# A decoder layer on one core: the mixer's output projection as seven products of quadrants instead of eight, and one weight split moved to the change of head pairs

## The chip, the cores and the metric

The kernel runs on one core of a Trainium2 chip, as one program. The metric is the time of the device in microseconds (us); lower is better. The profile was taken of one execution. TensorE (PE) multiplies, VectorE (DVE) and ScalarE (ACT) work on tiles in SBUF and PSUM, GpSimd (POOL) does small sums and issues some DMAs, SyncE (SP) issues most DMAs.

## The reference, cut to what matters

```python
def reference(x, mem, ...):
    h = rmsnorm(x, norm_mix_g)
    u_pool, q, k, v, f_logit, g_logit = jnp.split(h @ w_in, IN_SPLITS, axis=-1)
    y_pool = pool_mixer(u_pool, pool_w, pool_scale) @ w_pool_out
    y_fox = forgetting_attention(q, k, v, f_logit + b_forget) @ w_fox_out
    g_pool, g_fox = ...                                  # sigmoid gates, (1024, 1024) each
    x = x + (g_pool * y_pool + g_fox * y_fox) @ w_out    # the projection that is changed
    x = x + memory_cross_attention(rmsnorm(x), rmsnorm(mem), w_xq, w_xkv, w_xo)
    x = x + (silu(gt) * up) @ w_ffn_out                  # gt, up = rmsnorm(x) @ w_ffn_in
    return rmsnorm(x)
```

There are 1024 tokens, the model is 1024 wide, and all is float32. Call z = g_pool * y_pool + g_fox * y_fox. The changed product is z @ w_out, 1024 x 1024 by 1024 x 1024.

## The kernel before

Every float32 operand is kept as two parts, hi (a rounded copy, made by ACT) and lo (operand minus hi, made by DVE or POOL). `mm3` makes one product of a 128 x 128 tile by a 128 x 512 tile out of three matmuls: hi by lo, hi by hi, lo by hi.

z lies transposed, as eight tiles `gf[m]` of 128 model columns by 1024 tokens. For each pair j of tiles DVE multiplies the fox product in PSUM by the gate (L1780), adds the gated pool part `za[m]` (L1784), ACT rounds to `z_hi`, DVE subtracts to `z_lo` (L1464). PE meanwhile runs the fox products `fox_group(j, ...)`, 48 `mm3` thirds for one j.

The weights of all later products come in chunks of 128 x 1024 numbers, numbered through (`C_PO`, `C_FO`, `C_WO`, `C_XK`, ...). SP loads a chunk into one of two buffers `w_raw`, ACT makes `w_hi` (`split_hi`), DVE or POOL makes `w_lo` (`split_lo`), in one of three slots; the counter `w_used` says how many chunks PE has finished, and `lo_ready` how many are split. w_out takes eight chunks (`C_WO` to `C_WO + 7`), four for each half of the output columns; a chunk holds two of the eight k rows, and all eight token tiles use it: 48 matmuls (`tokens_by`). DVE then adds the eight banks of PSUM to the residual `xr` (L1799), a half of the columns at a time. When the fox products end (`w_used` reaches `C_WO`, 8) POOL issues the loads of `xr` (4 MB), then those of the memory tokens `mem_in`.

Every engine runs its instructions in the order of its block in the code. Waits are on semaphores. Nothing is reordered at run time.

The attention before it goes over 32 steps u (eight blocks of queries for each of four pairs of heads). A table, `SPLIT_AT`, says after which step a chunk is split on ACT: chunk 1 (the second of w_pool_out) at step 9. Its lo half is POOL's. A head pair ends at step 7.

The FFN of this kernel and its first projection already multiply by quadrants in Winograd's form, seven products P1 to P7, with sums S1 to S4 of the quadrants of the left operand and T1 to T4 of those of the right one.

Of the kernel before, what the change touches and what calls it, by code (L numbers as in the profile page):

```python
# [22 lines left out]
P = 128  # L23
S = 1024
# [34 lines left out]
C_XK = C_WO + 8  # L59
# [9 lines left out]
XO_ADDED = {tn: 2 * T + i + 1 for i, tn in enumerate(XO_ORDER)}  # L69
XO_OUT = {tn: 2 * (T - 1) + i + 1 for i, tn in enumerate(XO_ORDER)}  # L70
# [5 lines left out]
P1, P2, P3, P7, P5, P6, P4 = range(7)  # L76
PAIRS_F = 2 * NJ
# [65 lines left out]
SPLIT_AT = {5: 0, 9: 1, 12: 2, 18: 3, 23: 4, 28: 5, 32: 6}  # L143
# [73 lines left out]
def build(nc, x, mem, norm_mix_g, w_in, b_forget, b_gate, pool_w, pool_scale, w_pool_out,  # L217
# [15 lines left out]
    with ctx:  # L233
# [227 lines left out]
        def chunk_view(k):  # L461
            if k < C_FO:
                return cols(w_pool_out, 2 * (k - C_PO) * P, 2 * P)
            if k < C_WO:
                return cols(w_fox_out, 2 * (k - C_FO) * P, 2 * P)
            if k < C_XK:
                n, r = divmod(k - C_WO, 4)
                return rows(w_out, 2 * r, n * HALF)
# [9 lines left out]
            raise ValueError(k)  # L478

# [86 lines left out]
        def _(sp):  # L566
            def load_raw(n):
                if n >= RAWS:
                    sp.wait_ge(lo_ready, n - RAWS + 1)
# [142 lines left out]
            for n in range(SPLIT_AT[PAIRS * T] + 3, C_FF):  # L712
                load_raw(n)
# [70 lines left out]
        def _(pool):  # L784
# [660 lines left out]
        def _(dve):  # L1445
            def split_lo(n, lag=0):

                dve.wait_ge(hi_ready, n + 1)
# [318 lines left out]

            o_lo_of(PAIRS - 1)
            for j in range(4):
# [15 lines left out]
                for m in (2 * j, 2 * j + 1):  # L1785
                    dve.wait_ge(z_hi_ready, m + 1)
                    minus_hi(z_lo[:, m, :], gf[m][:], z_hi[:, m, :], z_lo_ready)

            def add(t, n, earlier, outs, used, turns=0):

                if t < T - 1:
                    dve.wait_ge(bank_out, turns * 28 + (outs + t + 1))
                else:
                    dve.wait_ge(w_used, turns * 12 + used)
                if earlier >= 2 * T:
                    dve.wait_ge(xr_added, turns * 32 + (earlier + t - 2 * T + 1))
                nc.vector.tensor_tensor(xr[:, t, half_of(n)], ps[:, t, :], xr[:, t, half_of(n)], ALU.add).then_inc(xr_added, 1)  # L1799

            for k in range(C_WO + 1, C_XK):
                split_lo(k + 2)
                if k == C_WO + 1:
                    for t in range(2):
                        normalise(N_MEM + t, xn_m[:, t, :], mem_in[:, t, :], 1, xn_ready)
                if k == C_WO + 3:
                    dve.wait_ge(xr_loaded, 16 * T)
                    for t in range(T):
                        add(t, 0, 0, 0, C_WO + 4)
                if k == C_WO + 4:  # L1810
                    for t in range(2):
                        xt_lo_of(XT_MEM + t, 2 * t, mt_hi[:, :, tile_of(t)], mt_lo[:, :, tile_of(t)])
                if k == C_WO + 7:
                    for t in range(T):
                        add(t, 1, T, T - 1, C_WO + 8)
# [312 lines left out]
        def _(pe):  # L2128
# [317 lines left out]

            def cross_tile(t):

                pe.wait_ge(xn_ready, N_CROSS + t + 1)
# [277 lines left out]
```

## Time and profile before

| what | value |
|---|---|
| median of 3 runs | 1457.88 us (1456.54 to 1458.14) |
| the profiled execution's own time | 1457.12 us |
| its span in the profile | 1455.2 us |
| PE busy | 1426.7 us, 98% |
| DVE, ACT, POOL busy | 976.4, 627.8, 488.7 us |
| PE in the stretch of the fox products and w_out (529 to 650 us) | busy throughout |

A matmul's duration in the profile is its time in the pipeline, 0.39 us for 512 columns; the next one starts 0.23 us after it. The distance of starts is what a matmul costs in a full stream, and busy time counts overlaps once. Where PE is busy throughout, time is won by fewer matmuls, if nothing else then makes it wait.

### The profile page before, as it was taken

To read this page: it belongs to the slowest core of one execution; us is meant where nothing else is said; L and a number is where in the kernel's file an instruction comes from. 1 tells how busy PE (TensorE), PEld (TensorE's weight loads), DVE (VectorE), ACT (ScalarE), POOL (GpSimd) and SP (SyncE) were. 2 spreads that over 40 slices of the span, in tenths; PEclk is the share of its full clock that TensorE was granted. 3 is DMA by queue.
4 is the path that set the end of the run, shared out by engine and by line. 5 is a ranking of instruction groups with operands and counts; after the bars stand their busy time and mean duration, and the time that the engine had idled before them with its cause. 6 is when DMAs were issued, how large, how long until landed. Compare 5 with 4: busy or idle time off the path is not lost.

```text
span 1455.2 us, 19228 instructions
## 1 busy us (share of the span) xinstructions
PE 1426.7 (98%) x7129; PEld 1174.6 (81%) x7129; DVE 976.4 (67%) x1394; ACT 627.8 (43%) x1183; POOL 488.7 (34%) x387
## 2 busy tenths in 40 slices
PE   7999999999999999999999999999999999999996
PEld 5878888887688788888888788888888888888885
DVE  7745594646866755327666887776777776795866
ACT  6545243427876642116543623333222233444444
POOL 5743233331110001005011654554444442354403
PEclk9999999999999999999999999999999999999998
DMA  8255263454332145114113213333332235873333
GB/s 211 65 113 128 47 152 73 82 114 167 102 102 95 44 159 202 59 44 145 30 44 116 73 58 109 109 109 109 109 108 89 101 109 209 309 269 95 90 106 131
DMA packets 104951, 166.88 MB, mean 115 GB/s; under 512 B 7277, under 2 KB 63105, under 8 KB 103450
## 3 DMA queue, kind: packets, MB, share of 16 engines
q1 hardware_dynamic: 98072, 145.55, 33.6%
q0 software_dynamic: 3200, 11.57, 2.2%
q10 hardware_dynamic: 3586, 8.52, 1.5%
q8 instruction: 58, 0.95, 0.3%
q14 instruction: 35, 0.29, 0.1%
HBM read 123.32 MB, written 42.30 MB: 114 GB/s over the span
## 4 chain that ended last, share of the span: by engine, by line
PE 88%; ACT 3%; DVE 3%; POOL 3%; issue 2%; DMA 0%; SPq 0%; DVEq 0%; POOLq 0%; ACTq 0%
PE ps L2132 27%; PE ps L2134 27%; PE ps L2133 27%; PE ps L2335 2%; PE ps L2344 2%; ACT prob L1212 1%; ACT prob_t L1203 1%; PE ps L2373 1%; PE ps L2374 1%; PE ps L2139 1%; DVE prob L1736 1%; POOL ms L799 1%; PE ps L2203 1%; PE ps L2510 0%; POOL rstd L802 0%
## 5 line engine op out<-in xcount | busy, mean ns | idle before, releaser
L2132 PE MATMUL ps<-t_lo,s_hi 128*128 128x512 f32 x308 | 119.9, 389 | 0.1
L2133 PE MATMUL ps<-t_hi,s_hi 128*128 128x512 f32 x308 | 119.8, 389 | 0.0
L2134 PE MATMUL ps<-t_hi,s_lo 128*128 128x512 f32 x308 | 119.8, 389 | 0.0
L1386 ACT ACTIVATE s_hi<-w_raw 128x512 fp32r<-128x512 f32 x77 | 48.7, 632 | 123.6 <-PE ps L2134 95.9
L2132 PE MATMUL ps<-h_lo_T,w_hi 128*128 128x512 f32 x256 | 100.5, 393 | 1.3 <-ACT u_t L1122 1.0
L1464 DVE TENSOR_TENSOR s_lo<-w_raw,s_hi 128x512 fp32r<-128x512 f32 x77 | 62.7, 814 | 57.4 <-ACT s_hi L1386 57.4
L2134 PE MATMUL ps<-h_hi_T,w_lo 128*128 128x512 f32 x256 | 99.7, 389 | 0.0
L2133 PE MATMUL ps<-h_hi_T,w_hi 128*128 128x512 f32 x256 | 99.6, 389 | 0.0
L1402 ACT ACTIVATE p_sb<-ps 128x512 f32<-128x512 f32 x22 | 13.1, 598 | 189.9 <-PE ps L2134 189.9
L810 POOL TENSOR_TENSOR w_lo<-w_raw,w_hi 128x1024 fp32r<-128x1024 f32 x11 | 27.7, 2519 | 188.8 <-ACT w_hi L1031 188.8
L2132 PE MATMUL ps<-hf_lo_T,w_hi 128*128 128x512 f32 x212 | 82.5, 389 | 0.0
L2133 PE MATMUL ps<-hf_hi_T,w_hi 128*128 128x512 f32 x212 | 82.5, 389 | 0.0
L2134 PE MATMUL ps<-hf_hi_T,w_lo 128*128 128x512 f32 x212 | 82.5, 389 | 0.0
L2132 PE MATMUL ps<-h_lo_B,w_hi 128*128 128x512 f32 x192 | 76.6, 399 | 2.3 <-DVE h_lo_B L1464 2.3
L2134 PE MATMUL ps<-h_hi_B,w_lo 128*128 128x512 f32 x192 | 75.3, 392 | 0.0
L2133 PE MATMUL ps<-h_hi_B,w_hi 128*128 128x512 f32 x192 | 75.2, 392 | 0.0
L1464 DVE TENSOR_TENSOR w_lo<-s_sum,w_hi 128x512 fp32r<-128x512 f32 x64 | 48.6, 764 | 39.1 <-ACT w_hi L1070 38.8
L1031 ACT ACTIVATE w_hi<-w_raw 128x1024 fp32r<-128x1024 f32 x32 | 33.9, 1059 | 90.4 <-PE ps L2134 86.6
L2132 PEld LDWEIGHTS ps<-t_lo,s_hi 128*128 128x128 f32 x308 | 57.8, 188 | 12.5 <-issue 0.5
L2133 PEld LDWEIGHTS ps<-t_hi,s_hi 128*128 128x128 f32 x308 | 57.8, 188 | 12.1
L2134 PEld LDWEIGHTS ps<-t_hi,s_lo 128*128 128x128 f32 x308 | 57.8, 188 | 11.9
L934 POOL TENSOR_TENSOR w_sum<-w_raw 128x512 f32<-128x512 f32 x11 | 14.5, 1321 | 156.5 <-DVE w_lo L1464 94.6
(380 smaller groups left out, 4248.2 us busy)
## 6 DMA issues: line engine op xcount, KB each, us to landing
w_raw<-hs_dram SPq DMA_DIRECT2D x77, 256.0 KB, 2.7
raw_p<-in_w_ffn_in SPq DMA_DIRECT2D x22, 512.0 KB, 4.5
w_raw<-in_w_ffn_in SPq DMA_DIRECT2D x22, 512.0 KB, 4.3
hs_dram<-h_sum SPq DMA_DIRECT2D x11, 1024.0 KB, 8.9
hs_dram<-hq SPq DMA_DIRECT2D x11, 768.0 KB, 7.0
wq_B<-in_w_ffn_out SPq DMA_DIRECT2D x8, 1024.0 KB, 8.0
raw_f<-in_w_in SPq DMA_DIRECT2D x14, 512.0 KB, 7.0
gate_dram<-c_st SPq DMA_DIRECT2D x28, 256.0 KB, 2.1
```

The source lines that it names most:

```text
L799: nc.gpsimd.tensor_scalar(ms[:, n:n + 1], ss[:, n:n + 1], 1.0 / D, EPS, ALU.mult, ALU.add).then_inc(ms_ready, 1)
L810: nc.gpsimd.tensor_tensor(w_lo[n % SLOTS][:], w_raw[n % RAWS][:], w_hi[n % SLOTS][:].bitcast(FP32), ALU.subtract).then_inc(lo_ready, 1)
L1031: nc.scalar.activation(w_hi[n % SLOTS][:], w_raw[n % RAWS][:], ACT.Copy).then_inc(hi_ready, 1)
L1203: nc.scalar.activation(prob_t[:, a, j0 * P:(j0 + n) * P], ps[:, 4 + g % 2, 0:n * P], ACT.Copy).then_inc(pt_copied, 1)
L1212: nc.scalar.activation(prob[u % 2][:, a, 0:n], prob[u % 2][:, a, 0:n], ACT.Exp, bias=neg_max[:, u % 2, a:a + 1], scale=-1.0, accum_out=pro ...
L1386: nc.scalar.activation(s2_hi[n % SLOTS2][:], s_raw(n % SLOTS2), ACT.Copy).then_inc(s_split_hi, 1)
L1464: nc.vector.tensor_tensor(out, a, hi.bitcast(FP32), ALU.subtract).then_inc(done, 1)
L2132: nc.tensor.matmul(dst, w_h, x_l, start=start, stop=False, skip_group_check=onto)
L2133: nc.tensor.matmul(dst, w_h, x_h, start=False, stop=False, skip_group_check=onto)
L2134: return nc.tensor.matmul(dst, w_l, x_h, start=False, stop=stop, skip_group_check=onto)
L2335: last = nc.tensor.matmul(ps[a * DH:(a + 1) * DH, 6, 0:P], v_sb[:, j, hc:hc + DH], prob_t[:, a, tile_of(j)], start=j == 0, stop=j == v % T)
L2344: last = nc.tensor.transpose(ps[:, 4 + g % 2, tile_of(j - j0)], prob[v % 2][:, a, tile_of(j)], ident[:])
```

## The change

z @ w_out is computed as seven products of 512 x 512 quadrants. A is z with its tokens halved (rows) and its model columns halved; B is w_out. With S1 = A21 + A22, S2 = S1 - A11, S3 = A11 - A21, S4 = A12 - S2 and T1 = B12 - B11, T2 = B22 - T1, T3 = B22 - B12, T4 = T2 - B21, the products are P1 = A11 B11, P2 = A12 B21, P3 = S4 B22, P4 = A22 T4, P5 = S1 T1, P6 = S2 T2, P7 = S3 T3, in the order P1, P2, P6, P5, P7, P3, P4. P6, P7 and P3 add up onto a bank that holds the product before. Each product takes two chunks, and a chunk serves four token tiles: 24 matmuls. So w_out has 14 chunks in place of 8, and the cross-attention's chunks are numbered from `C_XK = C_WO + 14`.

The sums T are POOL's: eight subtractions of 128 x 1024, out of quadrants that SP loads whole, 1 MB each (B12, B22, B11, B21). The sums S are DVE's: 16 operations of 128 x 512 (`z_total`). The counts of `wo_summed` and `z_sum` order them. The residual gets 32 additions of 128 x 512 in place of 16, and DVE and ACT split 14 chunks in place of 8. Chunk 1 is split at step 7 instead of 9. Core of the diff:

```diff
-C_XK = C_WO + 8
+C_XK = C_WO + 14
...
+WO_ORDER = (P1, P2, P6, P5, P7, P3, P4)
+WO_SUMS = {P6: "T2", P5: "T1", P7: "T3", P4: "T4"}
+WO_BANK_FREE = {P6: (1, 1), P5: (5, 1), P7: (9, 1), P3: (13, 1), P4: (18, 2)}
+Z_ADDED = (1, 2, 3, 4, 5, 6, 11, 12)
...
-SPLIT_AT = {5: 0, 9: 1, 12: 2, 18: 3, 23: 4, 28: 5, 32: 6}
+SPLIT_AT = {5: 0, 7: 1, 12: 2, 18: 3, 23: 4, 28: 5, 32: 6}
...
@@ SP
-            for n in range(SPLIT_AT[PAIRS * T] + 3, C_FF):
-                load_raw(n)
+            sp.wait_ge(z_sum, Z_ADDED[1])
+            load_quadrant("B12", wo_sums["T1"], 0, HALF)
+            load_raw(C_WO + 1)
+            sp.wait_ge(z_sum, Z_ADDED[3])
+            load_quadrant("B22", wo_sums["T2"], 4, HALF)
+            load_raw(C_WO + 2)
+            sp.wait_ge(w_used, C_WO)
+            load_quadrant("B11", wo_b11, 0, 0)
+            load_raw(C_WO + 3)
+            sp.wait_ge(z_sum, Z_ADDED[7])
+            load_quadrant("B21", wo_sums["T4"], 4, 0)
+            for n in range(C_WO + 4, C_FF):
+                if wo_product(n) not in WO_SUMS:
+                    load_raw(n)
@@ POOL
+            pool.wait_ge(z_sum, Z_ADDED[5])
...
+            for i in range(2):
+                nc.gpsimd.tensor_tensor(part_of(t3, i), part_of(t2, i), part_of(t1, i), ALU.subtract).then_inc(wo_summed, 1)
             pool.wait_ge(w_used, C_WO)
             for t in range(T):
                 pool.dma_start(xr[:, t, :], x2[tile_of(t), :]).then_inc(xr_loaded, 16)
-            pool.wait_ge(z_lo_ready, KD)
+            pool.wait_ge(wo_in["B11"][0], wo_in["B11"][1])
+            for i in range(2):
...
+                nc.gpsimd.tensor_tensor(part_of(t1, i), part_of(t1, i), part_of(wo_b11, i), ALU.subtract).then_inc(wo_summed, 1)
+            for i in range(2):
...
+                nc.gpsimd.tensor_tensor(part_of(t2, i), part_of(t2, i), part_of(t1, i), ALU.subtract).then_inc(wo_summed, 1)
             for t in range(2):
                 pool.dma_start(mem_in[:, t, :], mem2[tile_of(t), :]).then_inc(mem_loaded, 16)
             load_gain(norm_mem_g)
+            pool.wait_ge(wo_in["B21"][0], wo_in["B21"][1])
+            for i in range(2):
...
+                nc.gpsimd.tensor_tensor(part_of(t4, i), part_of(t2, i), part_of(t4, i), ALU.subtract).then_inc(wo_summed, 1)
@@ DVE
+            def z_total(q, k):
...
+                dve.wait_ge(z_sum, Z_SUMS[q, k] - 1)
+                dve.wait_ge(z_lo_ready, 4 + k + 1)
+                a11, a21, a12, a22 = (gf[i + k][:, half_of(h)] for i in (0, 4) for h in (0, 1))
+                a, b, op = {"S1": (a21, a22, ALU.add), "S2": (z_tile("S1", k), a11, ALU.subtract),
+                            "S3": (a11, a21, ALU.subtract), "S4": (a12, z_tile("S2", k), ALU.subtract)}[q]
+                nc.vector.tensor_tensor(z_tile(q, k), a, b, op).then_inc(z_sum, 1)
...
+                if j == 2:
+                    for q in ("S1", "S3"):
+                        for k in range(2):
+                            z_total(q, k)
...
+            for q, k in (("S2", 0), ("S2", 1), ("S1", 2), ("S1", 3), ("S2", 2), ("S2", 3)):
+                z_total(q, k)
+            split_lo(C_WO + 3)
+            z_lo_of("S2", range(2))
+            split_lo(C_WO + 4)
+            dve.wait_ge(xr_loaded, 16 * T)
+            for t in range(4):
+                add(0, 0, t, t, 0, t + 1, 0)
...
@@ PE
+            for n in range(C_WO, C_XK):
+                p, i = divmod(n - C_WO, 2)
+                q = WO_ORDER[p]
+                pe.wait_ge(lo_ready, n + 1)
+                pe.wait_ge(z_lo_ready, WO_LO[q] + 2 * i + 2)
...
+                for t in range(4):
+                    if i == 0 and q in WO_BANK_FREE:
+                        first, step = WO_BANK_FREE[q]
+                        pe.wait_ge(xr_added, first + step * t)
+                    for r in range(2):
+                        last = mm3(ps[:, bank + t, :], z_hi[:, k0 + 2 * i + r, tokens], z_lo[:, k0 + 2 * i + r, tokens],
+                                   w_hi[n % SLOTS][:, half_of(r)], w_lo[n % SLOTS][:, half_of(r)],
+                                   i == 0 and r == 0 and not onto, i == 1 and r == 1, onto)
```

The order on DVE, from the last two `z_lo` of the gated sums on. Before (z_hi, z_lo are z's parts, `w_lo2` the slot of chunk 11):

```order
L1464 TENSOR_TENSOR z_lo<-gf6,z_hi 128x1024
L1464 TENSOR_TENSOR z_lo<-gf7,z_hi 128x1024
L1451 TENSOR_TENSOR w_lo2<-w_raw1,w_hi2 128x1024
L1460 SCALAR_TENSOR_TENSOR xn_m<-mem_in,rstd,gain 128x1024 x2
L1451 TENSOR_TENSOR w_lo0<-w_raw0,w_hi0 128x1024
L1451 TENSOR_TENSOR w_lo1<-w_raw1,w_hi1 128x1024
```

The same place of the change:

```order
L1578 TENSOR_TENSOR z_lo<-gf6,z_hi 128x1024
L1578 TENSOR_TENSOR z_lo<-gf7,z_hi 128x1024
L1889 TENSOR_TENSOR gf0<-gf4,gf0 128x512
L1889 TENSOR_TENSOR gf1<-gf5,gf1 128x512
L1889 TENSOR_TENSOR gf6<-gf2,gf6 128x512
L1889 TENSOR_TENSOR gf7<-gf3,gf7 128x512
L1889 TENSOR_TENSOR za7<-gf6,gf2 128x512
L1889 TENSOR_TENSOR za7<-gf7,gf3 128x512
L1565 TENSOR_TENSOR w_lo2<-w_raw1,w_hi2 128x1024
L1578 TENSOR_TENSOR z_lo<-gf0,z_hi 128x512
L1578 TENSOR_TENSOR z_lo<-gf1,z_hi 128x512
L1565 TENSOR_TENSOR w_lo0<-wo_T2,w_hi0 128x1024
```

The lo half of chunk 11 (P2's second chunk) now stands behind six sums of quadrants, and that of chunk 12 (P6's first) behind two more subtractions.

POOL at the end of the fox products, before:

```order
L810 TENSOR_TENSOR w_lo2<-w_raw1,w_hi2 128x1024
L810 TENSOR_TENSOR w_lo0<-w_raw0,w_hi0 128x1024
L904 DMA xr<-in_x 128x1024 x8
L907 DMA mem_in<-in_mem 128x1024 x2
L910 DMA gain<-in_norm_mem_g 128x1024
```

The same place of POOL in the change:

```order
L886 TENSOR_TENSOR w_lo2<-w_raw1,w_hi2 128x1024
L886 TENSOR_TENSOR w_lo0<-w_raw0,w_hi0 128x1024
L989 TENSOR_TENSOR wo_T3<-wo_T2,wo_T1 128x1024 x2
L992 DMA xr<-in_x 128x1024 x8
L996 TENSOR_TENSOR wo_T1<-wo_T1,wo_b11 128x1024 x2
L999 TENSOR_TENSOR wo_T2<-wo_T2,wo_T1 128x1024 x2
L1001 DMA mem_in<-in_mem 128x1024 x2
L982 DMA gain<-in_norm_mem_g 128x1024
L1006 TENSOR_TENSOR wo_T4<-wo_T2,wo_T4 128x1024 x2
```

Eight subtractions of 128 x 1024 have come in around the DMA issues, where POOL issued DMAs only.

The attention steps on ACT where chunk 1 is split (`o_sb` is the output of the head pair that has ended, `q1_00` a part of a query block). Before:

```order
L1212 ACTIVATE prob1,prob_sum<-prob1,neg_max 128x256 x2
L1219 ACTIVATE d_hi<-ps,small 128x512 x2
L1078 ACTIVATE q1_00<-qk_st 64x512
L1080 ACTIVATE q1_00<-qk_st 64x512
L1031 ACTIVATE w_hi1<-w_raw1 128x1024
L1185 ACTIVATE o_sb<-ps 128x128
```

The same split in the change:

```order
L1300 ACTIVATE prob_t<-ps 128x384
L1309 ACTIVATE prob1,prob_sum<-prob1,neg_max 128x1024 x2
L1300 ACTIVATE prob_t<-ps 128x512
L1300 ACTIVATE prob_t<-ps 128x384
L1128 ACTIVATE w_hi1<-w_raw1 128x1024
L1282 ACTIVATE o_sb<-ps 128x128
```

It stood in a step that also prepares the next pair's q and k; now it stands ahead of the output of the pair that has ended.

## Rows read from the trace of the kernel before

**Rows 1.** The page: the span, and the busy time of PE.

```profile
span 1455.2 us, 19228 instructions
PE 1426.7 (98%) x7129; PEld 1174.6 (81%) x7129; DVE 976.4 (67%) x1394; ACT 627.8 (43%) x1183; POOL 488.7 (34%) x387
```

**Rows 2.** The page: the chain that ended last, by engine.

```profile
PE 88%; ACT 3%; DVE 3%; POOL 3%; issue 2%; DMA 0%; SPq 0%; DVEq 0%; POOLq 0%; ACTq 0%
```

**Rows 3.** Timeline of ACT, w_out: start, duration, what [idle before, releaser].

```profile
561.65 1.06 ACT L1031 ACTIVATE w_hi<-w_raw 128x1024 fp32r<-128x1024 f32 x1 [5.20 <-PE ps L2134]
...
572.53 1.06 ACT L1031 ACTIVATE w_hi<-w_raw 128x1024 fp32r<-128x1024 f32 x1 [5.19 <-PE ps L2134]
```

**Rows 4.** Timeline of ACT around attention steps 7 and 9.

```profile
374.83 0.28 ACT L1185 ACTIVATE o_sb<-ps 128x128 f32<-128x128 f32 x1 [2.24 <-PE ps L2335]
...
384.33 1.04 ACT L1031 ACTIVATE w_hi<-w_raw 128x1024 fp32r<-128x1024 f32 x1
```

**Rows 5.** Timeline of PE, step 12.

```profile
391.90 0.47 PE L2373 MATMUL ps<-k,q 128*128 128x512 f32 x1 [1.42 <-DVE neg_max L1736]
```

**Rows 6.** Timeline of DVE, pairs j = 2 and 3 of z.

```profile
555.35 2.36 DVE L1464 TENSOR_TENSOR z_lo<-gf,z_hi 128x1024 fp32r<-128x1024 f32 x2
...
562.75 1.23 DVE L1451 TENSOR_TENSOR w_lo<-w_raw,w_hi 128x1024 fp32r<-128x1024 f32 x1
563.89 2.35 DVE L1784 TENSOR_TENSOR gf<-gf,za 128x1024 f32<-128x1024 f32 x2
```

**Rows 7.** Timeline of POOL: two splits, and the DMA issues after the fox products.

```profile
492.22 2.38 POOL L810 TENSOR_TENSOR w_lo<-w_raw,w_hi 128x1024 fp32r<-128x1024 f32 x1 [25.41 <-ACT w_hi L1031]
...
561.86 4.23 POOL L904 DMA_DIRECT2D xr<-in_x  x8 [46.83 <-PE ps L2134]
568.89 1.05 POOL L907 DMA_DIRECT2D mem_in<-in_mem  x2 [2.81 <-DVE z_lo L1464]
...
659.96 3.33 POOL L810 TENSOR_TENSOR w_lo<-w_raw,w_hi 128x1024 fp32r<-128x1024 f32 x1
```

**Rows 8.** Timeline of DVE, at the two splits of rows 7.

```profile
493.12 2.56 DVE L1464 TENSOR_TENSOR o_lo<-o_sb,o_hi 128x1024 fp32r<-128x1024 f32 x1 [0.54 <-ACT o_hi L1189]
...
659.73 1.28 DVE L1460 SCALAR_TENSOR_TENSOR xn_x<-xr,rstd,gain 128x1024 f32<-128x1024 f32 x1
661.06 0.69 DVE L1464 TENSOR_TENSOR xk_lo<-ps,xk_hi 128x512 fp32r<-128x512 f32 x1
```

**Rows 9.** Timeline of POOL in the FFN: sums one behind the other.

```profile
1197.94 1.29 POOL L934 TENSOR_TENSOR w_sum<-w_raw 128x512 f32<-128x512 f32 x1 [15.40 <-DVE w_lo L1464]
...
1201.01 1.61 POOL L938 TENSOR_TENSOR w_sum<-w_raw,w_sum 128x512 f32<-128x512 f32 x1
```

**Rows 10.** Timeline of DVE beside them.

```profile
1201.40 1.77 DVE L1464 TENSOR_TENSOR late_lo<-w_raw,late_hi 128x512 fp32r<-128x512 f32 x1
1203.10 0.68 DVE L1991 TENSOR_TENSOR gbuf<-ps,p_sb 128x512 f32<-128x512 f32 x1
1203.70 1.18 DVE L1464 TENSOR_TENSOR late_lo<-w_raw,late_hi 128x512 fp32r<-128x512 f32 x1
```

**Rows 11.** DMA, 569 to 570 us: queue (q0 POOL's, q1 SP's): packets, MB, share.

```profile
q0 software_dynamic: 68, 0.23, 58.7%
q1 hardware_dynamic: 67, 0.14, 42.8%
```

**Rows 12.** SP's load of the chunk issued at 564.0 us.

```profile
L573 SPq DMA_DIRECT2D w_raw<-in_w_out x1: 368/368/368, 564.0 to 564.0; - x1
...
DMA to landing us min/median/max: 9.0/9.0/9.0
```

**Rows 13.** Stretches: window, length, busy of PE, PEld, DVE, ACT, POOL, granted clock, DMA.

```profile
14.00:16.00 2.00, 0.78 (x2) 0.72 (x3) 2.00 (x4) 1.13 (x3) 0.00 (x0) 0.80 0.86 303
16.00:18.00 2.00, 2.00 (x5) 1.11 (x4) 2.00 (x4) 0.67 (x1) 0.00 (x0) 0.50 1.03 412
18.00:20.00 2.00, 2.00 (x15) 1.88 (x15) 0.70 (x3) 1.37 (x4) 0.74 (x2) 0.85 1.02 396
```

More of the change, by code:

```diff
@@ L466, in chunk_view @@
             if k < C_XK:
-                n, r = divmod(k - C_WO, 4)
-                return rows(w_out, 2 * r, n * HALF)
+                k0, c0 = WO_ROWS[wo_product(k)]
+                return rows(w_out, k0 + 2 * (k % 2), c0)
             if k < C_XV:
@@ L900, in _, with part_of, load_gain @@
             split_lo(6)
+            def part_of(t, i):
+                return t[:, 2 * HALF * i:2 * HALF * (i + 1)]
+            def load_gain(g):
+                pool.dma_start(gain[:], g.broadcast_to([P, D])).then_inc(gain_in, 16)
+            t1, t2, t3, t4 = (wo_sums[q] for q in ("T1", "T2", "T3", "T4"))
+            pool.wait_ge(z_sum, Z_ADDED[5])
+            for q in ("B12", "B22"):
+                pool.wait_ge(wo_in[q][0], wo_in[q][1])
+            for i in range(2):
+                nc.gpsimd.tensor_tensor(part_of(t3, i), part_of(t2, i), part_of(t1, i), ALU.subtract).then_inc(wo_summed, 1)
             pool.wait_ge(w_used, C_WO)
@@ L1786, in _ @@
                     dve.wait_ge(z_hi_ready, m + 1)
[L1787 to L1794, printed above, removed]
-                else:
[L1796 to L1815, printed above, removed]
+                    to = slice(0, HALF if m < 4 else S)
@@ new lines, in _, with z_lo_of, add @@
+                    minus_hi(z_lo[:, m, to], gf[m][:, to], z_hi[:, m, to], z_lo_ready)
+                if j == 2:
+                    for q in ("S1", "S3"):
+                        for k in range(2):
+                            z_total(q, k)
+            def z_lo_of(q, ks=range(4)):
+                for k in ks:
+                    dve.wait_ge(z_hi_ready, Z_PARTS[q] + k + 1)
+                    minus_hi(z_part(z_lo, q, k), z_tile(q, k), z_part(z_hi, q, k), z_lo_ready)
+            def add(p, bank, t, xt, n, count, last, op=ALU.add):
+                if t < 3:
+                    dve.wait_ge(bank_out, 3 * p + t + 1)
+                else:
+                    dve.wait_ge(w_used, C_WO + 2 * p + 2)
+                if last:
+                    dve.wait_ge(xr_added, last)
+                half = xr[:, xt, half_of(n)]
+                nc.vector.tensor_tensor(half, half, ps[:, bank + t, :], op).then_inc(xr_added, 1)
@@ new lines, in _ @@
+            for q, k in (("S2", 0), ("S2", 1), ("S1", 2), ("S1", 3), ("S2", 2), ("S2", 3)):
[6 more added lines that the diff above has]
+                add(0, 0, t, t, 0, t + 1, 0)
+            z_lo_of("S2", range(2, 4))
+            split_lo(C_WO + 5)
+            for t in range(4):
+                add(1, 4, t, t, 0, 5 + t, t + 1)
@@ new lines, in _ @@
+            z_lo_of("S1")
+            split_lo(C_WO + 6)
+            for k in range(2, 4):
+                z_total("S3", k)
+            split_lo(C_WO + 7)
+            for t in range(4):
+                add(2, 0, t, t, 1, 9 + t, 0)
+            z_lo_of("S3")
+            split_lo(C_WO + 8)
+            for k in range(4):
+                z_total("S4", k)
+            for t in range(2):
+                normalise(N_MEM + t, xn_m[:, t, :], mem_in[:, t, :], 1, xn_ready)
+            split_lo(C_WO + 9)
@@ new lines, in _ @@
+            for t in range(4):
+                add(3, 4, t, 4 + t, 1, 13 + t, 0)
+            z_lo_of("S4")
+            split_lo(C_WO + 10)
+            split_lo(C_WO + 11)
+            for t in range(4):
+                add(4, 0, t, 4 + t, 1, 17 + 2 * t, 13 + t)
+                add(4, 0, t, 4 + t, 0, 18 + 2 * t, 0)
+            split_lo(C_WO + 12)
+            split_lo(C_WO + 13)
+            for t in range(4):
+                add(5, 4, t, t, 1, 25 + t, 9 + t)
+            split_lo(C_XK)
@@ L1817, in _ @@
+            for t in range(2):
+                xt_lo_of(XT_MEM + t, 4 + 2 * t, mt_hi[:, :, tile_of(t)], mt_lo[:, :, tile_of(t)])
+            split_lo(C_XK + 1)
+            for t in range(4):
+                add(6, 0, t, 4 + t, 0, 29 + t, 18 + 2 * t, ALU.subtract)
             for s in range(10):
```

153 lines of the change are left out of this document (107 added, 46 removed).

## The prediction

> **What bounds the kernel now.** I read the page first: PE is busy 98% of the span [rows 1], and the chain of what ended last runs 88% on PE, 3% each on ACT, DVE and POOL [rows 2]. So a matmul taken away is worth its whole distance of starts, as long as PE is then not made to wait. The second view was ACT's timeline in w_out: two `split_hi` start 10.88 us apart, and each had been idle for 5.2 us and was released by PE [rows 3]. One chunk is thus 48 matmuls in 10.88 us, 0.227 us each, and the splits follow PE, they do not lead it. The third was the attention around steps 7 and 9, where ACT has 2.24 us idle at one place and none at the other [rows 4], and PE waits 1.42 us a little later [rows 5]. The last were the timelines of DVE and POOL at the change from the fox products to w_out, and where both work at once [rows 6 to 10].
>
> **Term 1, the matmuls.** Eight products of quadrants are 384 matmuls, seven are 336: 48 x 0.227 = -10.88 us. Nothing of it is hidden, since PE is the path there.
>
> **Term 2, chunk 1.** At step 9 its `split_hi` stands in an unbroken run of ACT at 384.33 [rows 4]; DVE's maxima and with them PE's 1.42 us of waiting at 391.90 come out of that run [rows 5]. The operation lasts 1.04 us and costs 0.95 from start to start. Moved to step 7 it meets ACT while it waits 2.24 us for PE [rows 4], longer than it lasts, so it costs nothing there (0.95 if that idle time were gone). It is not missed: the chunk has long been loaded and is multiplied many steps later. Bounds: 0 (PE's wait comes from elsewhere) and -1.4 (the whole wait goes, since POOL's half of that split leaves DVE's way too). I take -0.95, ACT's own price.
>
> **Term 3, what DVE and POOL do at the joint.** This is the term that decides. POOL's subtraction of 128 x 1024 takes 2.38 us [rows 7], DVE's 1.23, and 1.15 from start to start [rows 6]. When both run at once with all operands in SBUF, one waits for the other: DVE's `o_lo` lasts 2.56 instead of 1.23 beside POOL's 2.38 [rows 7, 8]; POOL's `w_lo` at 659.96 lasts 3.33, which is 1.05 until DVE's `xn_x` is over (661.01) and 2.28 of its own [rows 7, 8]. DVE's next operation, which reads PSUM, keeps its 0.69 inside that POOL operation [rows 8]. In the FFN the two alternate, one for one, 1.6 to 1.77 us where 1.29 and 0.6 to 0.7 would do, and DVE's PSUM row between them takes 0.68 [rows 9, 10]. I count POOL at 2.3 for 1024 columns, DVE at 1.15, and at 0.60 for 512 (start to start at 1203.10 [rows 10]).
>
> The Trainium skill says the same of the cause ("SBUF — State Buffer", "Who interferes with whom"): the port pair that DVE and GpSimd share is locked for a whole instruction, and a `tensor_tensor` with one operand in PSUM stays out of it. The rows agree, with 3.33 = 1.05 + 2.28. By that rule the forecast stands; were the pair merely shared, rival D would come out.
>
> The line-up, in the clock of the profile of before. DVE's `z_lo` of pair 2 start at 555.35 [rows 6]; that releases POOL's T3. It is one for one from here: `z_lo` to 556.5, T3 to 558.8, `z_lo` to 559.95, T3 to 562.25. Four sums (4 x 0.6) and the gate products of pair 3 then end at 567.25, where before they ended at 562.75; `split_lo` of chunk 10 ends at 568.4 (PE wants it at 572.5, so it is met), the two gated sums at 570.7, `z_lo` 6 and 7 at 571.85 and 573.0.
>
> POOL's T1 waits for B11, whose load is issued when the fox products end, 561.65 by ACT's release [rows 3]. B11 is 1 MB in 512 packets of 2 KB, and `xr` travels beside it: in one microsecond each queue moves some 67 packets [rows 11]. From first bytes at about 563.6 that is 7.6 us or a little more: B11 is in at about 571.8. A chunk issued at 564.0 there landed after 9.0 us [rows 12]; the raw chunk 11 behind B11 lands at about 576, so its `w_hi` is ready at 577 and is not what comes last.
>
> From 573.0 on DVE has six sums of 512 before `split_lo` of chunk 11, and POOL has T1, T1, T2, T2, DMA issues (1.05 for two and a little for the gain [rows 7]), T4, T4. One for one: four POOL operations and six sums, 573.0 + 4 x 2.3 + 6 x 0.6 + 0.1 = 585.9. One T4 gets in ahead of the split, + 2.3 + 1.15 = 589.35. PE starts w_out at 561.65, P2's first chunk 10.88 (P1) later at 572.53, and wants chunk 11 a further 5.44 later, at 577.97. It stands still for 11.4 us. Without POOL beside it, DVE's six sums (3.6) and the split (1.15) would end at 577.75, with no wait. If only the raw chunk's landing held, the wait would be at most 1 us. So the bounds of this term are 0 and, with both T4 ahead, 13.7; I take +11.4, since rows 7 to 10 show the exclusion wherever both work at once.
>
> **Term 4, PE's clock after the standstill.** Near the start, after a wait, PE's granted clock falls from the level of 2.4 GHz to that of 1.2: 0.80, 0.50, 0.85 in three stretches of 2 us [rows 13]. What is missing from 1 is (0.20 + 0.50 + 0.15) x 2 = 1.7 us. A wait of 11 us is longer than any in w_out before, so I add +1.7; bounds 0 and 1.7.
>
> **What costs nothing.** After chunk 11 PE takes 24 x 0.227 = 5.44 us for a chunk. Per chunk DVE has one split (1.15) and up to four adds from PSUM (4 x 0.69, unhindered by POOL [rows 8]), 3.9 together, and ACT 1.06: six more splits on each and 16 more adds lie under PE's 76.2 us. Gone that cover, they would be 6 x 1.15 + 16 x 0.69 = 18 us. The waits of P6 for banks are met: the adds begin right after the split of chunk 12, at about 592, and P6 starts no earlier than 594.8. The quadrants B12 and B22 are issued long before they are used. POOL's `mem_in` issues come some 15 us later than at 568.89 [rows 7], ahead of T4 and still some 20 us before PE turns to the memory tokens' transposes. The start of the cross-attention keeps its distances to w_out's end.
>
> **The sum.** -10.88 - 0.95 + 11.4 + 1.7 = +1.3. The profiled execution took 1457.12, so 1458.4; the median of the runs is 0.76 above that one: **1459.2 us**. What a measurement can tell from no change is 0.2%, 2.9 us.
>
> **Rivals.**
> - *A, as above* (0.45): one T4 ahead of the split, wait of 10.6 to 11.5, clock 0 to 1.7. Own range 1456.5 to 1460.
> - *B, slower* (0.25): B11 is in before DVE starts `z_lo` 7 (571.85, against my 571.8; the estimate is good to 1.5 us). POOL's T1 slips in ahead of it, everything on POOL comes one turn earlier, and both T4 pass before the split: 591.65, a wait of 13.7. -10.88 - 0.95 + 13.7 + 1.7 = +3.6: 1461.5. With the clock's 1.7, it is slower by over 0.2% from a wait of 13.0 on. For it speaks that `xr` may start slowly; against it that SP's queue has a share of 43% only, and POOL's 59%, in [rows 11].
> - *C, faster* (0.15): B11 lands late, at 575.5 or later (the 9.0 us for half as much in [rows 12] speak for it). Most sums are then done before T1 starts; two or three POOL operations stand ahead of the split, wait about 6.7: 1457.88 - 10.88 - 0.95 + 6.7 + 1.7 = 1454.5.
> - *D, faster* (0.15): POOL and DVE hold each other up less than in [rows 7 to 10], because each of them waits elsewhere in between, or they share and both get slower: the work of 573.0 to 577.75 doubled is a wait of 4.8, or none. 1457.88 - 10.88 - 0.95 + 4.8 + 1.7 = 1452.6, down to 1446.1 with neither wait nor clock.
> - That the product saves no matmuls can be left out: PE's order has 48 fewer.
>
> **Numbers.** B's top and the clock's bound give 1462.5. Down to 1450 leaves out the part of D in which hardly a wait is left, about 0.1, and above 1462.5 about 0.07. Faster by over 0.2% are C and D, 0.30; within it A, 0.45; slower B, 0.25.
>
> **What would show it.** PE idle before the matmuls of chunk 11, released by DVE's `w_lo`, 11 us: term 3. DVE's sums of 512 there lasting 2.9 us in place of 0.7, alternating with POOL's T1 and T2: the exclusion; sums of 0.7 would be D, T1 starting after them C, two T4 ahead of the split B. Granted clock of 0.5 after the gap: term 4. ACT's split of chunk 1 in idle time at step 7, and PE's wait at step 12 down to 0.5: term 2. w_out's matmuls 76.2 us long plus the wait: term 1. The prediction is wrong if PE waits elsewhere in w_out, for a bank, a quadrant sum T or a raw chunk, which I priced at nothing.

## The result, and the profile of the changed kernel

The changed kernel takes 1460.59 us (median of 17 runs, 1459.22 to 1461.65), the kernel before 1457.55 us (17 runs, 1456.10 to 1458.43): ratio 1.0020, 95% interval 1.0014 to 1.0027. It is 3.0 us slower, at the edge of the 0.2% within which I had called it no change (forecast 1459.2, range 1450.0 to 1462.5).

The page of the changed kernel: span, busy time, and the chain that ended last, by engine.

```profile
span 1458.6 us, 19271 instructions
...
PE 1419.7 (97%) x7081; PEld 1168.2 (80%) x7081; DVE 1020.6 (70%) x1448; ACT 641.3 (44%) x1205; POOL 511.5 (35%) x395
...
PE 86%; DVE 5%; ACT 3%; POOL 3%; issue 2%; DMA 0%; SPq 0%; DVEq 0%; POOLq 0%; ACTq 0%
```

PE has 48 matmuls fewer and 7.0 us less to do [rows 1], and DVE holds 5% of the chain in place of 3% [rows 2]. The 48 matmuls are 10.9 us of stream. The busy time fell by less for two reasons: part of w_out now runs at a lower clock (1.7 us, below), and in the first 560 us, ahead of w_out, PE is busy for 548.7 us in this profile and for 546.9 in that of before. PE's timeline in w_out has one wait (start, duration, what [idle before, releaser]):

```profile
590.94 0.80 PE L2300 MATMUL ps<-w_lo,z_hi 128*128 128x512 f32 x1 [12.93 <-DVE w_lo L1565]
```

This is the first matmul of chunk 11; it waited for DVE's `split_lo`. From start to start PE loses 13.1 us (the matmul before it started at 577.61 and the usual distance is 0.23). DVE's timeline from the split of chunk 10 to that of chunk 11:

```profile
567.21 3.14 DVE L1565 TENSOR_TENSOR w_lo<-w_raw,w_hi 128x1024 fp32r<-128x1024 f32 x1
570.27 6.75 DVE L1907 TENSOR_TENSOR gf<-gf,za 128x1024 f32<-128x1024 f32 x2
576.95 4.53 DVE L1578 TENSOR_TENSOR z_lo<-gf,z_hi 128x1024 fp32r<-128x1024 f32 x2
581.40 6.90 DVE L1889 TENSOR_TENSOR gf<-gf 128x512 f32<-128x512 f32 x4
588.33 1.42 DVE L1889 TENSOR_TENSOR za<-gf 128x512 f32<-128x512 f32 x2
589.66 1.22 DVE L1565 TENSOR_TENSOR w_lo<-w_raw,w_hi 128x1024 fp32r<-128x1024 f32 x1
```

And POOL's over the same stretch:

```profile
555.57 6.73 POOL L989 TENSOR_TENSOR wo_T<-wo_T 128x1024 f32<-128x1024 f32 x2 [40.41 <-DVE gf L1907]
562.24 4.21 POOL L992 DMA_DIRECT2D xr<-in_x  x8
566.88 5.72 POOL L996 TENSOR_TENSOR wo_T<-wo_T,wo_b 128x1024 f32<-128x1024 f32 x2 [0.43 <-DMA wo_b<-in_w_out]
572.56 6.70 POOL L999 TENSOR_TENSOR wo_T<-wo_T 128x1024 f32<-128x1024 f32 x2
...
582.31 5.44 POOL L1006 TENSOR_TENSOR wo_T<-wo_T 128x1024 f32<-128x1024 f32 x2 [1.50 <-DMA wo_T<-in_w_out]
```

Read the two side by side. A split or sum of 1024 columns costs DVE 1.15 us alone [rows 6]; here the split of chunk 10 lasts 3.14 and the two gated sums 6.75, while POOL's two T2 take 6.70 where POOL alone needs 4.6. The two gated sums last 3.41 and 3.42 us, which is 1.15 and one whole operation of POOL: that is the picture of [rows 7 to 10]. With the two T3, each of POOL's eight operations stands in DVE's way once. From 581.40 the six sums and the split take 9.4 us; alone they are 3.6 + 1.15, and the two turns of T4 are the rest.

PE's clock after the gap: window, length, busy of PE, PEld, DVE, ACT, POOL, granted clock, DMA.

```profile
588.00:590.00 2.00, 0.00 (x0) 0.00 (x0) 1.93 (x4) 0.85 (x2) 0.00 (x0) 0.50 0.00 0
590.00:592.00 2.00, 1.06 (x3) 0.87 (x4) 2.00 (x3) 2.00 (x3) 0.00 (x0) 0.50 0.01 3
592.00:594.00 2.00, 2.00 (x6) 1.62 (x5) 2.00 (x4) 0.31 (x1) 0.00 (x0) 0.50 0.79 255
594.00:596.00 2.00, 2.00 (x9) 1.59 (x8) 2.00 (x4) 0.00 (x0) 0.00 (x0) 0.93 0.01 4
```

The granted clock is at the level of 1.2 GHz when PE starts again, and what is lost until it is back at 2.4 is 1.06 x 0.5 + 2 x 0.5 + 2 x 0.07 = 1.7 us.

At the other place, attention, ACT's split of chunk 1 stands at 373.64 behind the preceding step's work, with 1.29 us of idle time still left after it, and PE's wait at step 12 is 0.58 in place of 1.42 [rows 5].

```profile
373.64 1.05 ACT L1128 ACTIVATE w_hi<-w_raw 128x1024 fp32r<-128x1024 f32 x1
375.98 0.28 ACT L1282 ACTIVATE o_sb<-ps 128x128 f32<-128x128 f32 x1 [1.29 <-PE ps L2503]
```

```profile
391.88 0.47 PE L2541 MATMUL ps<-k,q 128*128 128x512 f32 x1 [0.58 <-DVE neg_max L1850]
```

The two profiles differ by 1.15 us before attention step 7 as well, at code that is the same in both; among the profiles of this study PE reaches that place between 371.4 and 374.6 us. So single profiles are compared here stretch by stretch, and whole kernels by their medians.

### The profile page after: what moved, and what is told of

The parts are those of the page before. It is cut to its first block, busy times and chain, and to the rows that moved or that the text cites. A ratio compares the mean times of both kernels' runs of the same rounds, so it can differ in the third digit from the quotient of the medians.

```text
span 1458.6 us, 19271 instructions
## 1 busy us (share of the span) xinstructions
PE 1419.7 (97%) x7081; PEld 1168.2 (80%) x7081; DVE 1020.6 (70%) x1448; ACT 641.3 (44%) x1205; POOL 511.5 (35%) x395
## 4 chain that ended last, share of the span: by engine, by line
PE 86%; DVE 5%; ACT 3%; POOL 3%; issue 2%; DMA 0%; SPq 0%; DVEq 0%; POOLq 0%; ACTq 0%
PE ps L2300 26%; PE ps L2302 26%; PE ps L2301 26%; PE ps L2503 2%; PE ps L2512 2%; ACT prob L1309 1%; ACT prob_t L1300 1%; PE ps L2541 1%; DVE gf L1889 1%; PE ps L2542 1%; PE ps L2307 1%; DVE gf L1907 1%; POOL ms L875 1%; PE ps L2371 1%; DVE prob L1850 0%
## 5 line engine op out<-in xcount | busy, mean ns | idle before, releaser
L1578 DVE TENSOR_TENSOR s_lo<-w_raw,s_hi 128x512 fp32r<-128x512 f32 x77 | 59.5, 773 | 63.3 <-ACT s_hi L1500 63.3
L2159 DVE TENSOR_TENSOR hq<-ps,p_sb 128x512 f32<-128x512 f32 x11 | 7.6, 690 | 85.8 <-DMA hs_dram<-h_sum 64.8
```

The source lines that it names most:

```text
L1578: nc.vector.tensor_tensor(out, a, hi.bitcast(FP32), ALU.subtract).then_inc(done, 1)
```

## Experiments

The theory: DVE and POOL shut each other out whenever both run an operation whose inputs all lie in SBUF, and POOL's eight sums T are paid turn by turn on DVE's way to chunk 11. The rivals: the six sums S that stand ahead of the split are the cause by themselves; a landing (B11, B21, the raw chunk) is; or the engines share and both slow down, without shutting out. All experiments were timed beside the kernel before; 1457.52 was its median beside the first four, 1457.08 beside the next four and 1457.10 beside the last two.

**POOL's sums made small.** T1, T2 and T4 work on 8 columns of 1024, so the output is not the reference's. T3 stays whole. The edit of T1, with T2 and T4 alike:

```diff
-nc.gpsimd.tensor_tensor(part_of(t1, i), part_of(t1, i), part_of(wo_b11, i), ALU.subtract)
+nc.gpsimd.tensor_tensor(part_of(t1, i)[:, 0:8], part_of(t1, i)[:, 0:8], part_of(wo_b11, i)[:, 0:8], ALU.subtract)
```

> POOL's T1, T2 and T4 work on 8 of 1024 columns, so the output is not the reference's; T3, every load, wait and count stay. If the wait before chunk 11 (12.9 us, 1460.6 in all) comes from DVE and POOL shutting each other out, DVE's six sums run in 3.6 us, chunk 11 is split by 578 and the wait is 0 to 1 us: 1457.55 - 10.88 - 1.0 = 1445.7, up to 1446.7. If it comes from the six sums standing ahead of the split, or from the landing of B11, B21 or the raw chunk, PE still waits 8 us or more and the time is 1456 or above. If both engines only share a port, half the wait stays: 1451.

Measured: 1445.52 us, ratio 0.9925 (0.9912 to 0.9937). PE's one wait in w_out, and DVE's six sums and split:

```profile
580.00 0.50 PE L2300 MATMUL ps<-w_lo,z_hi 128*128 128x512 f32 x1 [0.49 <-DVE w_lo L1565]
```

```profile
574.49 2.87 DVE L1889 TENSOR_TENSOR gf<-gf 128x512 f32<-128x512 f32 x4
577.39 1.42 DVE L1889 TENSOR_TENSOR za<-gf 128x512 f32<-128x512 f32 x2
578.73 1.22 DVE L1565 TENSOR_TENSOR w_lo<-w_raw,w_hi 128x1024 fp32r<-128x1024 f32 x1
```

Every load, wait and place is as in the change; only the length of T1, T2 and T4 is gone, and 15 us with it. The order on DVE and the landings alone leave a wait of 0.5 us, so these two rivals fall. This run does not exclude that the engines share and both slow down. The durations above do: at half speed the gated sums would last 2.3 us, and they last 3.41 and 3.42.

**The split moved, alone and undone.** The change with chunk 1 at step 9, and the kernel before with it at step 7.

```diff
-SPLIT_AT = {5: 0, 7: 1, 12: 2, 18: 3, 23: 4, 28: 5, 32: 6}
+SPLIT_AT = {5: 0, 9: 1, 12: 2, 18: 3, 23: 4, 28: 5, 32: 6}
```

> The change with chunk 1 split at step 9 again. If the move to step 7 is worth what the two traces show between steps 7 and 12 (PE 1.0 to 1.2 us earlier), this is 1.0 slower than the change: 1461.6. If the move was worth nothing and the difference is in other stretches, it is equal to the change: 1460.6.

> The kernel before with chunk 1 split at step 7. If the move by itself is worth 1.0: 1456.6. If not: 1457.6.

Measured: 1461.89 (ratio to before 1.0028, 1.0017 to 1.0039), 1.3 above the change; and 1456.40 (0.9992, 0.9983 to 1.0001), 1.1 below the kernel before. PE's wait at step 12 with the split at step 9 and the new projection:

```profile
392.96 0.47 PE L2541 MATMUL ps<-k,q 128*128 128x512 f32 x1 [1.42 <-DVE neg_max L1850]
```

and with the split at step 7 and the old projection:

```profile
391.98 0.47 PE L2373 MATMUL ps<-k,q 128*128 128x512 f32 x1 [0.59 <-DVE neg_max L1736]
```

The wait goes with the split, whatever the projection. Neither timing alone is clear of no difference by its interval; the two differences agree with each other and with the rows, so I take the move to be worth about 1.1 us.

**The split of chunk 11 ahead of the six sums.**

```diff
+            split_lo(C_WO + 3)
             for q, k in (("S2", 0), ("S2", 1), ("S1", 2), ("S1", 3), ("S2", 2), ("S2", 3)):
                 z_total(q, k)
-            split_lo(C_WO + 3)
```

> The change with DVE's split of chunk 11 ahead of the six sums. If DVE and POOL shut each other out, z_lo 7 still ends at 581.5 behind T2, the split ends at about 583 and PE waits some 5 us there, then some 5 us more for P6's first chunk, whose sums now stand behind: about 10 in place of 12.9, 1457.5. If the order on DVE is the whole cause, the wait goes and nothing takes its place: 1447 to 1449.

Measured: 1458.47, ratio 1.0009 (1.0000 to 1.0018). PE's waits in w_out:

```profile
582.32 0.80 PE L2300 MATMUL ps<-w_lo,z_hi 128*128 128x512 f32 x1 [4.65 <-DVE w_lo L1565]
594.35 0.77 PE L2300 MATMUL ps<-w_lo,z_hi 128*128 128x512 f32 x1 [4.05 <-DVE xr L1932]
```

One wait of 12.9 has become two of 4.65 and 4.05, and the clock falls after each. The forecast was 1457.5, 1.0 lower: it had counted the two waits, but not that the clock is paid for twice. The order alone gives back 2.1 us: `z_lo` 7, behind four turns of POOL, still holds chunk 11 up, and what stood ahead of the split now holds up P6.

**T4 only after the split.** POOL waits for the split of chunk 11 before it makes T4; DVE's order is that of the change.

```diff
             pool.wait_ge(wo_in["B21"][0], wo_in["B21"][1])
+            pool.wait_ge(lo_ready, C_WO + 4)
```

> POOL makes T4 only once chunk 11 is split, all else as in the change. By the exclusion the six sums (581.4 to 588) run unhindered, the split ends at 586.2 and the wait is 8.3 in place of 12.9; T4 then holds z_lo of S2 up by two turns, which P6 may feel by up to 2: 1456 to 1458. If T4 beside the sums is of no account: 1460.6.

Measured: 1455.84, ratio 0.9991 (0.9982 to 1.0000).

```profile
585.38 0.79 PE L2301 MATMUL ps<-w_lo,z_hi 128*128 128x512 f32 x1 [9.12 <-DVE w_lo L1566]
```

The wait is 3.8 shorter; two turns of 2.3 were forecast. The time is 0.2 below the forecast's range (1456 to 1458), since P6 felt nothing of the later T4. It is 4.75 below the change, for two POOL instructions that start some 5 us later, counted from the start of w_out (ACT's release: 560.04 here, 561.78 in the change; T4: 585.46 against 582.31).

**T1 only after the split.** Chunk 11 is split first, as in the run with the split first (that part of the edit is not shown again), and POOL's T1 waits for it.

```diff
             pool.wait_ge(wo_in["B11"][0], wo_in["B11"][1])
+            pool.wait_ge(lo_ready, C_WO + 4)
```

> Chunk 11 is split ahead of the six sums, and POOL starts T1 only when that is done. By the exclusion z_lo 7 ends at 573 and the wait before chunk 11 is 0 to 1. T1, T2 (9.2 us, with turns of DVE between) then come just ahead of P6's first chunk, wanted at 583.4 and ready at 587 to 589: one wait of 4 to 6 there and 1 of clock, 1450.5 to 1453. If POOL's sums do not hold up DVE, this equals the kernel with the split first alone: 1458.5, or worse by the later T2.

Measured: 1460.44, ratio 1.0021 (1.0012 to 1.0030): a miss. PE's one wait, and DVE's sums:

```profile
595.66 0.76 PE L2301 MATMUL ps<-w_lo,z_hi 128*128 128x512 f32 x1 [12.35 <-DVE xr L1933]
```

```profile
573.97 9.09 DVE L1890 TENSOR_TENSOR gf<-gf 128x512 f32<-128x512 f32 x4
583.09 8.95 DVE L1890 TENSOR_TENSOR za<-gf 128x512 f32<-128x512 f32 x2
```

Chunk 11 came without a wait, as expected. But I had counted four POOL turns ahead of P6 and forgotten T4: six POOL operations stand among six DVE sums, 18.0 us for 3.6 of DVE's own, and P6 waits 12.35 for what comes behind them. The time by itself fits the rival that I had named (1458.5, or worse by the later T2); the sums' durations decide against it, since unhindered they would take 3.6. What was wrong was the count of the turns, and the turns are not strictly one for one either. The first sum lasts 0.68 and the next four 2.7 to 2.8, but the last starts at 585.85 and lasts 6.20: both T4 (586.84 to 591.48) run in it, one directly behind the other. Why it did not end before they began, at 586.84, isn't shown.

**B11 late.** The raw chunk 11 first, B11 only once chunk 10 is split.

```diff
-            load_quadrant("B11", wo_b11, 0, 0)
             load_raw(C_WO + 3)
+            sp.wait_ge(lo_ready, C_WO + 3)
+            load_quadrant("B11", wo_b11, 0, 0)
```

> B11 is issued behind the raw chunk 11 and only when chunk 10 is split (568.4), so it lands at 573.5 to 574.5, as late as the forecast had it or later, in place of 566.9. Counting turns from there: z_lo 7 ends at 573.0, four POOL sums stand among the six of DVE, the split ends at 586 to 587: a wait of 8 to 9 with the clock's 1.7, 1455.7 to 1457.5. If the landing of B11 is of no account, 1460.6.

Measured: 1454.95, ratio 0.9986 (0.9977 to 0.9995), 0.75 below the forecast's range, and by another way. B11 was there at 579.6, not at 574: issued at 568.8, behind POOL's `xr`, it landed after 10.8 us. All six sums and the split were done before T1 began, and the wait moved to P6:

```profile
579.62 4.93 POOL L997 TENSOR_TENSOR wo_T<-wo_T,wo_b 128x1024 f32<-128x1024 f32 x2 [12.84 <-DMA wo_b<-in_w_out]
```

```profile
578.80 0.50 PE L2301 MATMUL ps<-w_lo,z_hi 128*128 128x512 f32 x1 [0.47 <-DVE w_lo L1566]
590.98 0.76 PE L2301 MATMUL ps<-w_lo,z_hi 128*128 128x512 f32 x1 [6.44 <-DVE xr L1933]
```

A load that lands some 12.4 us later, counted from the start of w_out, makes the kernel 5.6 us faster than the change. The two numbers are those of rival C of the prediction (1454.5, wait 6.7), but not its mechanism, so the agreement is in part luck: C had two or three POOL operations ahead of the split and the wait before chunk 11. Here T1, T2 and T4 all come behind the split, and P6 waits because T1 and T2, which it needs, are made late.

**The six sums made small.** They work on 8 of 512 columns, so the output is not the reference's; POOL is as in the change.

```diff
-nc.vector.tensor_tensor(z_tile(q, k), a, b, op).then_inc(z_sum, 1)
+w = 8 if Z_SUMS[q, k] in range(13, 19) else HALF
+nc.vector.tensor_tensor(z_tile(q, k)[:, 0:w], a[:, 0:w], b[:, 0:w], op).then_inc(z_sum, 1)
```

> DVE's six sums ahead of the split work on 8 of 512 columns, so the output is not the reference's; POOL as in the change. z_lo 7 still ends at 581.5 behind T2, the sums take 0.5 and the split ends at 583.3: a wait of 5.4 in place of 12.9, and turns for T4 after it that P6 may feel by up to 2: 1453 to 1455. If the sums' own 3.6 us were all their price, the wait would be 9.3: 1457.

Measured: 1456.31, ratio 0.9997 (0.9988 to 1.0006); a wait of 7.8, between the two numbers (5.4 and 9.3), and a time above the range of 1453 to 1455. The sixth sum still waited for a turn of POOL:

```profile
581.25 0.76 DVE L1890 TENSOR_TENSOR gf<-gf 128x8 f32<-128x8 f32 x4
582.04 2.47 DVE L1890 TENSOR_TENSOR za<-gf 128x8 f32<-128x8 f32 x2
584.44 1.21 DVE L1565 TENSOR_TENSOR w_lo<-w_raw,w_hi 128x1024 fp32r<-128x1024 f32 x1
```

The first four take 0.76 together and the fifth 0.17; the sixth takes 2.27, because POOL has begun T4 at 582.15, just before its own start at 582.24. In this run the price of a turn did not shrink with the operation that waits.

**All sums T on DVE.** POOL issues DMAs only; ACT splits chunk 12 before the hi parts of S2. DVE's order behind the last `z_lo` of z:

```diff
-            for q, k in (("S2", 0), ("S2", 1), ("S1", 2), ("S1", 3), ("S2", 2), ("S2", 3)):
-                z_total(q, k)
             split_lo(C_WO + 3)
+            wo_total("T1", 0)
+            wo_total("T2", 0)
+            for k in range(2):
+                z_total("S2", k)
+            split_lo(C_WO + 4)
             z_lo_of("S2", range(2))
-            split_lo(C_WO + 4)
             dve.wait_ge(xr_loaded, 16 * T)
             for t in range(4):
                 add(0, 0, t, t, 0, t + 1, 0)
+            for q, k in (("S1", 2), ("S1", 3), ("S2", 2), ("S2", 3)):
+                z_total(q, k)
+            wo_total("T1", 1)
+            wo_total("T2", 1)
             z_lo_of("S2", range(2, 4))
             split_lo(C_WO + 5)
```

(`wo_total(q, i)` makes half i of a sum T; T3 stands behind S1 and S3 in pair 2 of z, T4 behind the split of chunk 16.)

> All eight sums T on DVE (1.15 us each) and none on POOL; DVE splits chunk 11 before the sums, T1 and T2 are made half by half, the first halves ahead of P6's first chunk, T4 later; ACT splits chunk 12 before z_hi of S2. If POOL's sums beside DVE are the cause, DVE's 9.2 us more of own work still leave it ahead of PE: waits of 0 to 1 us, 1445.6 to 1447. If DVE is simply overloaded at this place, its extra 9.2 us lengthen the wait: 1460 or more.

Measured: 1450.58, ratio 0.9956 (0.9943 to 0.9968). The same work on the busier engine is 10.0 us faster than in the change. The forecast (1445.6 to 1447) was too low by 3.6 to 5.0: PE waits once, before chunk 13, and pays for it in clock as well (last section). DVE had been idle before that, for the raw chunk 11 and for `xr`:

```profile
591.90 0.79 PE L2303 MATMUL ps<-w_lo,z_hi 128*128 128x512 f32 x1 [3.34 <-DVE w_lo L1546]
```

```profile
572.08 1.23 DVE L1546 TENSOR_TENSOR w_lo<-w_raw,w_hi 128x1024 fp32r<-128x1024 f32 x1 [1.47 <-ACT w_hi L1108]
...
581.85 2.48 DVE L1927 TENSOR_TENSOR xr<-xr,ps 128x512 f32<-128x512 f32 x4 [2.48 <-DMA xr<-in_x]
```

**The same, with DVE's two idle stretches filled.**

```diff
-            split_lo(C_WO + 3)
             wo_total("T1", 0)
             wo_total("T2", 0)
+            split_lo(C_WO + 3)
...
             z_lo_of("S2", range(2))
+            wo_total("T1", 1)
+            wo_total("T2", 1)
+            for k in range(2, 4):
+                z_total("S1", k)
             dve.wait_ge(xr_loaded, 16 * T)
             for t in range(4):
                 add(0, 0, t, t, 0, t + 1, 0)
-            for q, k in (("S1", 2), ("S1", 3), ("S2", 2), ("S2", 3)):
-                z_total(q, k)
-            wo_total("T1", 1)
-            wo_total("T2", 1)
+            for k in range(2, 4):
+                z_total("S2", k)
```

> The sums T on DVE in another order: T1 and T2 first halves in the 1.5 us in which DVE waits for the raw chunk 11, their second halves and S1 in the 2.5 us in which it waits for xr. The wait of 3.3 us before chunk 13 goes, with its 1.7 us of slow clock: 1450.6 - 3.3 - 1.7 = 1445.6, or 1445.1 worked out from the kernel before (1457.1 - 10.9 - 1.1). If the wait before chunk 13 has another cause (a bank, a raw chunk), it stays at 1450.6.

Measured: 1446.95, ratio 0.9931 (0.9918 to 0.9943). It beats the kernel before by 10.2 us and the change by 13.6. The forecast (1445.1 to 1445.6) was still too low, by 1.4 to 1.9 us. Three short waits are left in w_out, all for a `w_lo` of DVE:

```profile
594.17 0.50 PE L2305 MATMUL ps<-w_lo,z_hi 128*128 128x512 f32 x1 [0.16 <-DVE w_lo L1546]
611.14 0.50 PE L2305 MATMUL ps<-w_lo,z_hi 128*128 128x512 f32 x1 [0.34 <-DVE w_lo L1546]
617.08 0.50 PE L2305 MATMUL ps<-w_lo,z_hi 128*128 128x512 f32 x1 [0.20 <-DVE w_lo L1546]
```

Counted from start to start against the usual 0.227, these three places and one at 588 cost some 1.8 us (my estimate from PE's timeline), about the size of the gap. The granted clock is 1.00 throughout w_out. DVE, now with the sums T as well, is at these places just behind PE.

## Why the prediction was right, and where it was not

The sign and the balance came out: seven products save 10.9 us, and a new wait with its clock gives all of it back. The difference was low, though: +1.3 forecast, +3.0 measured. The time came out nearer, 1.4 us off, because the median before that I started from (3 runs) is 0.3 us above that of the 17 runs. Step by step:

- **Term 1** (-10.88): right. Between ACT's release at the start of w_out and at its end lie 88.84 us before (561.65 to 650.49) and 92.75 in the change (561.78 to 654.53). The difference, +3.9, is -10.88 + 13.1 + 1.7, with nothing left over. The two ends, before and in the change:

```profile
650.49 1.06 ACT L1031 ACTIVATE w_hi<-w_raw 128x1024 fp32r<-128x1024 f32 x1 [9.82 <-PE ps L2134]
```

```profile
654.53 1.06 ACT L1128 ACTIVATE w_hi<-w_raw 128x1024 fp32r<-128x1024 f32 x1 [3.48 <-PE ps L2302]
```

- **Term 2** (-0.95): right, as far as can be told: 1.1 and 1.3 in the two runs, and 0.84 less wait at step 12.
- **Term 3** (+11.4): the mechanism was right, the size was low by 1.7: 13.1. The step that failed is the landing of B11, "in at about 571.8". It landed 5.1 us after its issue, at 566.9. I had taken the 67 packets a microsecond of each queue from a stretch in which both were under way [rows 11]; here SP's load was issued first, and in the microsecond from 565 its queue moved 0.41 MB, `xr` nothing. Why `xr`, issued from 562.2 on, had not begun by then isn't shown.

```profile
q1 hardware_dynamic: 199, 0.41, 104.7%
```

So T1 and T2 took their four turns ahead of `z_lo` 6 and 7, which ended at 581.4 and not at 573.0, and both T4 came ahead of the split. That is rival B, told with chance 0.25: its wait of 13.7 and 1461.5 against 13.1 and 1460.6. B had T1 one turn early and not all of T1 and T2, but its count holds: the likeliest case had seven POOL operations ahead of the split, the trace shows eight. That the landing decides is shown by the run with B11 late.
- **Term 4** (+1.7): the size was met, 1.7 by the windows, but in part by luck, and its bound was wrong. [rows 13] give only 1.5 when each stretch is weighted with PE's busy time (0.78 of the first 2 us). The fall of the clock that they show is not in the profile of the change, where the same place runs at 1.00. And in the run with the split at step 9 the same wait (12.96) was followed by a loss of 2.3. Where PE waits twice it is paid twice: in the run with the split first, the stretches behind 4.65 us and behind 4.05 us both begin at 0.50. The place of [rows 13] in the change (window, length, busy of PE, granted clock, DMA):

```profile
16.00:18.00 2.00, 2.00 (x6) 1.00 1.01 412
```

- **The rivals.** D (little exclusion) fell by the durations of 3.4 us in the change, and by the 15 us that the small sums on POOL gave. "What costs nothing" held: P6, P7, P3 and P4 waited for no bank, quadrant or raw chunk in the change.

The four terms as measured, -10.88 - 1.1 + 13.1 + 1.7, come to +2.8 of the +3.0. My range of the likeliest case, 1456.5 to 1460, missed the time by 0.6; the whole range held it.

## What to carry to other kernels

Before a sum is given to the engine that has time, ask which operations of the other engine it will shut out, and who waits for those: POOL was idle here, and yet each sum that it made put some 2.3 us on DVE's way to PE, twice the 1.15 that the same sum costs on DVE. Count turns, not microseconds: how many POOL operations are ready before the DVE instruction that PE waits for; a transfer that lands early can add one. Eight subtractions cost DVE 9.2 us of its own; made there, with the orders of DVE and ACT adapted, they moved the kernel from 0.2% slower to 0.7% faster. How much of that is the order alone wasn't run with the sums left on POOL. The best of the runs that leave them there took 1454.95, and the small sums on POOL show what their length costs: 15 us.

## What the runs showed of the hardware

A DVE operation of 8 columns waited as long for POOL (2.27 us in all) as one of 1024. It goes the other way round too: with the sums on POOL made small, its two T2 of 8 columns lasted 2.34 us together beside DVE's split and gated sum of 1.2 each, where the two T1 took 0.36. The turns went one for one in the change, but not always: with T1 late a sum of 512 columns lasted 6.20 us over both T4, and with B11 late a `z_lo` of 512 columns that started at 592.55 lasted 3.48, while the two T4 (590.74 to 595.47) followed each other directly. Of two DMA queues whose first transfers were issued half a microsecond apart (561.7 and 562.2), the first had all the bandwidth at 565 us, and only later did they share. The same load of 1 MB landed after 5.1 us there, and after 10.8 us when it was issued at 568.8, with `xr` under way.

What the clock costs did not grow with the wait. Behind nine waits I added up PE's busy time times what is missing from a granted clock of 1, by windows:

| wait, us | run | lost, us |
|---|---|---|
| 12.9 | the change | 1.7 |
| 13.0 | split at step 9 | 2.3 |
| 12.35 | T1 late | 2.5 |
| 9.1 | T4 late | 2.4 |
| 7.8 | the six sums small | 2.6 |
| 6.4 | B11 late | 1.6 |
| 4.65 | split first | 2.4 |
| 4.05 | split first | 1.5 |
| 3.3 | sums T on DVE | 3.0 |

Behind the waits of 0.5 us and less, in three of the kernels, the clock stayed at 1.00. The largest loss stands behind the shortest wait of the table, because PE was held at half speed for longer after it started again at 591.9 (window, length, busy of PE, granted clock, DMA):

```profile
592.00:594.00 2.00, 2.00 (x5) 0.50 0.03 8
594.00:596.00 2.00, 2.00 (x6) 0.50 0.00 0
596.00:598.00 2.00, 2.00 (x7) 0.53 0.00 0
```

Why one restart is followed by a longer slow stretch than the other, these runs don't settle; two waits of 12.9 and 13.0 in the same place differ by 0.6 us. My bound of 1.7 for this term was taken from a single place and was no bound.
